# Bias tables built through a DRAM matrix of repeated rows inside the delta rule, and attention run from wide to narrow dilation

## The chip, the cores and the metric

The kernel runs on one core of a Trainium2 chip. The time is device microseconds (us) for one execution. The core has five instruction streams: TensorE (PE, matrix products into PSUM), VectorE (DVE), ScalarE (ACT), GpSimd (POOL) and SyncE (SP). SP and ACT each own a queue on which they issue DMAs; both queues are served by the same 16 DMA engines.

## The reference

One decoder block on 2048 tokens of width 1024, all float32. The change touches two of its parts, which share only their input and are joined by the output projection:

```python
# gated delta rule, 4 heads of 128, a scan over chunks
u = u0_c - w_c @ state;  o = qg_c @ state + aqk_c @ u;  state = gl_c * state + kg_c.T @ u
# attention, 8 heads of 64, three branches (window, dilation) = (128, 1), (512, 4), (2048, 16)
delta = qi + 128 - kj                       # qi < 128, kj < 256
bias = rel_bias[t5_bucket(max(delta, 0) * dil)]
s = q @ k.T * dh ** -0.5 + bias;  s = where(valid, s, -1e30);  o_i, lse_i = softmax parts
ob = sum over branches of softmax(lse) * o_i, then RMSNorm
x = x + gate * (concat([oa, ob]) @ w_out)
```

The bias of a branch depends on `qi - kj` alone: a 128 x 256 table per head whose row is the row above it, shifted by one.

## The kernel before, in words

The program is a row of phases (`PHASES`). Each has its own SBUF tiles and semaphores (`Room`), with a barrier of all engines behind it. The engines follow orders written out by hand and wait on semaphores; there is no scheduler. Four phases matter here.

**The delta rule** (`deltanet`) goes over the 2048 tokens in 16 chunks of 128. SP loads each chunk's operands into two alternating buffers, about one chunk ahead: `nt`, `kg`, `qg`, `aqk`, `vb`, `z` (256 KB each, rows of 2 KB), `kc` (256 KB in rows of 512 B) and eight DMAs of 128-byte rows into the diagonal blocks of `dz` and `dzt` (L941, L942). In chunks 0 to 7 SP also loads 1 MB of the attention's q and k into `big` (L987). For each chunk PE runs eleven groups of 128x128 products (L1023, L1075, L1076), DVE masks and subtracts, ACT copies `u` out of PSUM (L1105) and squares the output, and POOL scales it; SP stores it (L968). The chunks form a chain through `state`.

**The bias tables** (`bias_tables`) come next, as a phase of their own. SP loads the 32x8 bias weights and two constants. One product per branch selects the bucket for each of 384 distances (L1217); DVE adds the mask (L1230), which gives one row of 384 numbers per head and branch, on 8 partitions. The rows go to DRAM in one small DMA (L1207). Three DMAs of 1 MB read them back with the same distance step for each partition, so that the table arrives upside down (L1211); PE turns it over by a product with a flipped identity (L1222), and DVE copies it out of PSUM (L1233).

**Attention** (`attention`) has 48 units of 128 queries, 16 for each branch. `RUNS` sets the order: dilation 1, then 4, then 16. A unit with `False` has 128 keys, one with `True` has 256. POOL gathers strided q and k, SP loads v (L1310, L1313) and stores the unit's output to `o_d` (L1320), and ACT issues the 4 MB load of `w_out` at the start (L1420).

**The output projection** (`mix_out`) reads for each tile of 128 tokens the delta rule's output (`mo_y`) and the three branches' outputs (`mo_o`, 792 KB), weights and normalises them, and multiplies by `w_out`. SP loads tiles 0 and 1 at its start, behind two constants.

Of the kernel before, what the change touches and what calls it, by code (L numbers as in the profile page):

```python
# [880 lines left out]
def deltanet(nc, m, a):  # L881
# [5 lines left out]
    with Room(nc, "gd") as R:  # L887
# [20 lines left out]
        nrm = R.sb("nrm", [P, NT, 2 * GH])  # L908
        pool_self, dve_self = R.plain("pool_self"), R.plain("dve_self")
# [16 lines left out]
        with R.block() as block:  # L926
# [93 lines left out]
            def _(pe):  # L1020
# [57 lines left out]

                fifth_y(0)
# [15 lines left out]
            def _(act):  # L1095
                act.wait_ge(*eps_set.n(1))
                nc.scalar.activation(nrm[:, :, :], m.ssq[:, :, :], ACT.Sqrt, bias=eps[:, :]).then_inc(*nstd_ready.inc)
                act.wait_ge(*nrm_ready.n(2))
                for c in range(NT):
                    b = c % 2  # L1100
                    act.wait_ge(*u_done.n(c + 1))
# [13 lines left out]
                    nc.scalar.activation(st[:, b, :], st[:, b, :], ACT.Sqrt, bias=eps[:, :], scale=1.0 / P).then_inc(*std_ready.inc)  # L1115

            @block.vector
            def _(dve):
# [52 lines left out]

                masked(0, 0, L5)
# [14 lines left out]
def bias_tables(nc, m, a):  # L1187

    with Room(nc, "bt") as R:
        rel = R.sb("rel", [NE, AH])
        hot = R.sb("hot", [NE, NB * BIAS_W])
        off = R.sb("off", [AH, NB * BIAS_W])
        rows = R.sb("rows", [AH, NB * BIAS_W])
        flip = R.sb("flip", [P, NB, AH, 2 * P])
        small_in, rows_out, flip_in = R.sig("small_in", 16), R.sig("rows_out", 16), R.sig("flip_in", 16)
        rows_done, rows_ready, done, read = R.sig("rows_done"), R.sig("rows_ready"), R.sig("done"), R.sig("read")
        ps = m.ps
        with R.block() as block:  # L1200
            @block.sync
            def _(sp):
                sp.dma_start(rel[:, :], a["rel_bias"]).then_inc(*small_in.inc)
                sp.dma_start(hot[:, :], a["bucket_one"]).then_inc(*small_in.inc)
                sp.dma_start(off[:, :], a["bucket_off"]).then_inc(*small_in.inc)
                sp.wait_ge(*rows_ready.n(NB))
                sp.dma_start(m.bias_d, rows[:, :]).then_inc(*rows_out.inc)  # L1207
                sp.wait_ge(*rows_out.n(1))
                for n in range(NB):
                    src = bass.AP(m.bias_d.tensor, n * BIAS_W, [[1, P], [NB * BIAS_W, AH], [1, 2 * P]])  # L1210
                    sp.dma_start(flip[:, n, :, :], src).then_inc(*flip_in.inc)  # L1211

            @block.tensor
            def _(pe):
                pe.wait_ge(*small_in.n(3))
                for n in range(NB):
                    nc.tensor.matmul(ps[0:AH, n, 0:BIAS_W], rel[:, :], hot[:, n * BIAS_W:(n + 1) * BIAS_W], start=True, stop=True).then_inc(*rows_done.inc)  # L1217
                pe.wait_ge(*flip_in.n(NB))
                for n in range(NB):
                    pe.wait_ge(*read.n(n))  # L1220
                    for h in range(0, AH, 2):
                        last = nc.tensor.matmul(ps[:, 4 + h // 2, :], m.cst[:, C_FLIP:C_FLIP + P], flip[:, n, h:h + 2, :].rearrange("p h k -> p (h k)"), start=True, stop=True)  # L1222
                    last.then_inc(*done.inc)

            @block.vector
            def _(dve):
                for n in range(NB):
                    dve.wait_ge(*rows_done.n(n + 1))
                    s = slice(n * BIAS_W, (n + 1) * BIAS_W)
                    nc.vector.tensor_tensor(rows[:, s], ps[0:AH, n, 0:BIAS_W], off[:, s], ALU.add).then_inc(*rows_ready.inc)  # L1230
                for n in range(NB):
                    dve.wait_ge(*done.n(n + 1))
                    nc.vector.tensor_copy(m.bias[:, n, :, :].rearrange("p h k -> p (h k)"), ps[:, 4:8, :].rearrange("p b n -> p (b n)")).then_inc(*read.inc)  # L1233


def attention(nc, m, a):
# [6 lines left out]
        (0, 0, 1, (False,), lambda i, j: 0),  # L1243
        (1, 0, NT // 2 - 1, (True, True), lambda i, j: i * (2 * P) + (1 + j) * P),
        (NT - 1, 0, 1, (True,), lambda i, j: (NT - 1) * P),
        (NT, 1, BR[1][0], (False, True, True, True), lambda i, j: i + j * BR[1][0] * P),
        (2 * NT, 2, BR[2][0] // 2, (False, False), lambda i, j: i * 2 + j),
# [36 lines left out]
    with Room(nc, "at") as R:  # L1284
        qk = m.qk
        qb = R.sb("qb", [P, 2, STEPS, P])
# [7 lines left out]
        later_in = R.sig("later_in", 16)  # L1294
# [5 lines left out]
        with R.block() as block:  # L1300
            @block.sync
            def _(sp):
                for unit, prev in units(sp):
                    if unit:
# [6 lines left out]
                        else:  # L1311
                            src = bass.AP(m.v_d.tensor, first * AW, [[dil * AW, P], [1, AW]])
                            sp.dma_start(v[:, b, 1, :], src).then_inc(*v_in[b].inc)  # L1313
                    if prev:
# [6 lines left out]
                for b in range(2):  # L1321
                    sp.wait_ge(*out[b].n(UNITS // 2))
# [830 lines left out]
class Shared:  # L2153
    pass


def attention_part(nc, m, a):

    with nc.sbuf_tensor("bias", [P, NB, AH, 2 * P], F32) as m.bias:
        bias_tables(nc, m, a)  # L2160
# [99 lines left out]
```

## Time and profile before

| | |
|---|---|
| median of 3 runs | 2684.2 us (2676.27 to 2690.61) |
| profiled execution | 2681.78 us, of it span 2679.9 us |
| PE busy | 2272.5 us (85%) |
| DVE / ACT / POOL busy | 1104.7 / 805.8 / 329.6 us |
| DMA | 426.63 MB, mean 159 GB/s |
| delta rule | from 968 to 1154 us |
| bias tables | from 1155.55 us to 1198.59 us |
| attention | from 1199.3 to 1557 us |
| output projection, first SP issue | 1560.68 us |

The profile gives the time each engine is busy, who released it from a wait, and for the DMAs the number of packets, their bytes, and the share of 16 engines' time that the packets took. In these traces a packet is one contiguous row of a transfer; a DMA adds one small packet per DMA engine used. `issue` as a releaser means that the profile shows nothing that the engine waited for. Times in a timeline are counted from the start of the span.

### The profile page before, as it was taken

How to read it: one execution, taken by the hardware profiler on the slowest of the kernel's cores; microseconds unless marked ns; L12 is line 12 of the kernel's file. 1: busy time of each engine (PE TensorE's matmuls, PEld its weight loads, DVE VectorE, ACT ScalarE, POOL GpSimd, SP SyncE). 2: the span in 40 equal slices, each digit the busy share in tenths (PEclk: the TensorE clock that was granted, in tenths of full speed). 3: DMA queues.
4: the chain of work that ended last, by engine and by line, in shares of the span. 5: the costliest groups of instructions: out<-in, count | busy, mean ns of one | idle time of the engine just before them, and what ended most of it. 6: DMA issues, size and time to landing. Idle time of an engine off the chain costs nothing. (4 is left out here: it accounts for less than half of the span.)

```text
span 2679.9 us, 31777 instructions
## 1 busy us (share of the span) xinstructions
PE 2272.5 (85%) x9218; PEld 1329.4 (50%) x9219; DVE 1104.7 (41%) x2029; ACT 805.8 (30%) x2123; POOL 329.6 (12%) x314
## 2 busy tenths in 40 slices
PE   3999899999888978949999959999169999999940
PEld 2666444444444458926777735555024444444410
DVE  5444132322346525526788845654501111111127
ACT  1433111111333112216777834442011111111125
POOL 0000000000111014411133400000310000000022
PEclk9999999999999989969999979999579999999975
DMA  8443011112456549723233333331058766579767
GB/s 337 146 135 135 33 55 63 55 63 87 137 176 194 176 130 296 237 97 115 95 88 95 104 110 127 127 127 44 5 186 308 242 229 218 202 265 328 270 249 283
DMA packets 178532, 426.63 MB, mean 159 GB/s; under 512 B 41824, under 2 KB 77920, under 8 KB 162960
## 3 DMA queue, kind: packets, MB, share of 16 engines
q1 hardware_dynamic: 153664, 335.37, 36.9%
q0 software_dynamic: 12832, 43.02, 4.7%
q10 hardware_dynamic: 11952, 47.19, 4.3%
q8 instruction: 45, 0.74, 0.1%
q14 instruction: 39, 0.32, 0.0%
HBM read 304.44 MB, written 121.07 MB: 159 GB/s over the span
## 5 line engine op out<-in xcount | busy, mean ns | idle before, releaser
L627 PE MATMUL ps<-big,pc_w 128*128 128x512 f32 x1280 | 556.8, 596 | 10.1 <-DMA pc_w<-in_w_chan 10.1
L627 PEld LDWEIGHTS ps<-big,pc_w 128*128 128x128 f32 x1280 | 243.3, 191 | 310.5 <-issue 299.5
L1976 PE MATMUL ps<-ex_wgu,ex_xt 128*128 x800 | 359.1, 602 | 24.2 <-DMA ex_wgu<-in_w_gate_up 23.5
L1976 PEld LDWEIGHTS ps<-ex_wgu,ex_xt 128*128 128x128 f32 x800 | 150.3, 193 | 198.9 <-issue 198.9
L310 PE MATMUL ps<-cp_wt,big 128*128 128x344 f32 x768 | 225.5, 454 | 0.0
L1562 PE MATMUL ps<-w_out,mo_yt 128*128 128x512 f32 x512 | 225.0, 598 | 0.0
L1372 PE MATMUL ps<-at_v,at_pt 128*128 128x128 f32 (+1 forms) x1200 | 183.1, 290 | 6.2 <-DMA at_v<-v_d 6.2
L1986 PE MATMUL ps<-ex_wd,ex_hidt 128*128 x400 | 181.8, 598 | 4.3 <-issue 2.9
L310 PEld LDWEIGHTS ps<-cp_wt,big 128*128 128x128 f32 x768 | 145.9, 191 | 76.9 <-issue 4.1
L1434 ACT ACTIVATE at_p<-at_p,at_low 128x256 f32<-128x256 f32 (+1 forms) x384 | 174.0, 456 | 20.1 <-DVE at_low L1401 19.7
L1372 PEld LDWEIGHTS ps<-at_v,at_pt 128*128 128x128 f32 x1200 | 149.1, 191 | 52.8 <-issue 35.7
L2058 DVE TENSOR_TENSOR ex_hid<-ex_sg,ps 128x256 f32<-128x256 f32 x50 | 21.1, 421 | 362.1 <-ACT ex_sg L2026 340.1
L1562 PEld LDWEIGHTS ps<-w_out,mo_yt 128*128 128x128 f32 x512 | 97.2, 192 | 116.5 <-issue 116.5
L1399 DVE SCALAR_TENSOR_TENSOR at_p<-ps,bias 128x512 f32<-128x512 f32 (+1 forms) x192 | 109.3, 569 | 69.9 <-PE ps L1347 69.4
L2047 DVE TENSOR_TENSOR ex_y<-ps,mod 128x1024 f32<-128x1024 f32 x50 | 61.2, 1225 | 174.6 <-PE ps L1986 174.6
L2026 ACT ACTIVATE ex_sg<-ps 128x256 f32<-128x256 f32 x50 | 19.3, 386 | 356.7 <-PE ps L1976 356.7
L1347 PE MATMUL ps<-at_kb,at_qb 64*128 64x256 f32 (+1 forms) x768 | 119.5, 389 | 6.1 <-POOL at_kb L1333 5.1
L1949 POOL DMA_INDIRECT ex_xg<-h_d,ex_idx x50 | 47.3, 945 | 545.9 <-DVE ex_idx L2050 499.2
L1417 ACT COPY at_pt<-ps 128x512 f32<-128x512 f32 (+1 forms) x192 | 93.8, 488 | 66.5 <-PE ps L1357 61.1
L782 DVE TENSOR_SCALAR pc_cv<-pc_pre,pc_wc 128x2048 f32<-128x2048 f32 x12 | 15.4, 1287 | 234.5 <-ACT pc_pre L707 234.5
L1401 DVE TENSOR_REDUCE at_low<-at_p 128x2 f32<-128x512 f32 (+1 forms) x192 | 109.4, 570 | 6.6
L1986 PEld LDWEIGHTS ps<-ex_wd,ex_hidt 128*128 128x128 f32 x400 | 72.7, 192 | 78.2 <-issue 78.2
(289 smaller groups left out, 2866.5 us busy)
## 6 DMA issues: line engine op xcount, KB each, us to landing
ex_wgu<-in_w_gate_up SPq DMA_DIRECT2D x32, 2048.0 KB, 11.1
ex_wd<-in_w_down SPq DMA_DIRECT2D x32, 1024.0 KB, 7.8
ys_d<-ex_y ACTq DMA_DIRECT2D x50, 512.0 KB, 8.0
cp_w<-in_w_ada SPq DMA_DIRECT2D x24, 1024.0 KB, 5.4
ch_d<-pc_cv SPq DMA_DIRECT2D x20, 1024.0 KB, 3.9
at_v<-v_d SPq DMA_DIRECT2D x27, 512.0 KB, 3.9
o_d<-at_o SPq DMA_DIRECT2D x48, 264.0 KB, 2.1
mo_o<-o_d SPq DMA_DIRECT2D x16, 792.0 KB, 6.6
```

What stands on the lines that cost most here:

```text
L310: last = nc.tensor.matmul(ps[:, ROW_A + g, 0:THIRD], m.ht[:, k, t * P:(t + 1) * P], wt[:, k, g * THIRD:(g + 1) * THIRD], start=(k == 0), s ...
L627: last = nc.tensor.matmul(ps[:, n % 2, :], w[:, ch % 2, k, :], m.ht[:, k, g * BANK:(g + 1) * BANK], start=(k == 0), stop=(k == KD - 1))
L1347: last = nc.tensor.matmul(ps[:, 2 * (s % 2) + h, lo:2 * P], qb[r, b, s, :], kb[r, b, s, lo:], start=True, stop=True)
L1372: last = nc.tensor.matmul(ps[:, 6 + b, w], pt[:, e, h, k, :], v[:, b, k, w], start=(k == k0), stop=(k == 1))
L1399: nc.vector.scalar_tensor_tensor(p[:, s, :, lo:], ps[:, 2 * e:2 * e + 2, lo:2 * P], DH ** -0.5, m.bias[:, unit[0][1], 2 * s:2 * s + 2, lo: ...
L1401: nc.vector.tensor_reduce(low[:, b, 2 * s:2 * s + 2], p[:, s, :, lo:], AX.X, ALU.max, negate=True).then_inc(*max_ready[e].inc)
L1417: nc.scalar.copy(pt[:, e, :, k:, :], ps[:, 4 + e, :].rearrange("p (h k n) -> p h k n", h=2, k=2)[:, :, k:, :]).then_inc(*pt_ready[e].inc)
L1434: ins = nc.scalar.activation(p[:, s, h, lo:], p[:, s, h, lo:], ACT.Exp, bias=low[:, b, at:at + 1], accum_out=low[:, b, at + AH:at + AH + 1])
L1562: last = nc.tensor.matmul(ps[:, 2 + 2 * b + n, :], yt[:, b, k, :], w[:, k, n * BANK:(n + 1) * BANK], start=(k == 0), stop=(k == KD - 1))
L1976: last = nc.tensor.matmul(ps[:, 2 + b, :], xt[:, b, k, :], wgu[:, bass.ds(half * WGU + k * 2 * DE, 2 * DE)], start=(k == 0), stop=(k == KD ...
L1986: last = nc.tensor.matmul(ps[:, 6 + n, :], hidt[:, b, k, :], wd[:, bass.ds(half * WD + (k * D + n * BANK), BANK)], start=(k == 0), stop=(k ...
L2047: nc.vector.tensor_tensor(y[:, b, :], ps[:, 6:8, :].rearrange("p n w -> p (n w)"), gate, ALU.mult).then_inc(*y_ready[b].inc)
```

## The change

The bias phase goes. Its work moves into the delta rule, and the turning over by PE and DVE is replaced by DRAM traffic: `bias_d` grows from one row per head and branch to 128 copies of it (3 x 8 x 128 x 384 floats, 4.72 MB), written by ACT from 8 partitions. A read whose step from partition to partition is one less than the row length then takes from each copy a window that starts one element earlier, and gives the table the right way up; ACT issues these three reads (1 MB each) ahead of chunks 5, 6 and 7. The tables lie in an SBUF tile that lives from the delta rule to the output projection; it holds the constants and rows first.

```diff
 deltanet, PE, in read_state and ahead of fifth_y(0):
+                    if c == 0:
+                        pe.wait_ge(*rows_ready.n(NB))
+                def bias_rows():
+                    pe.wait_ge(*table_in.n(3))
+                    for n in range(NB):
+                        last = nc.tensor.matmul(ps[0:AH, KS + n, 0:BIAS_W], rel[:, :], hot[...], start=True, stop=True)
+                    last.then_inc(*rows_done.inc)
+                bias_rows()
                 fifth_y(0)
 deltanet, ACT:
+                act.dma_start(rel[:, :], a["rel_bias"]).then_inc(*table_in.inc)
+                act.dma_start(hot, a["bucket_one"]).then_inc(*table_in.inc)
+                act.dma_start(off, a["bucket_off"]).then_inc(*table_in.inc)
                 nc.scalar.activation(nrm[:, :, :], m.ssq[:, :, :], ACT.Sqrt, bias=eps[:, :])
+                act.wait_ge(*rows_ready.n(NB))
+                for n in range(NB):
+                    act.dma_start(m.bias_d[n], rows[:, n * BIAS_W:(n + 1) * BIAS_W].unsqueeze(1).to_broadcast([AH, P, BIAS_W])).then_inc(*rows_out.inc)
                 for c in range(NT):
+                    if 5 <= c < 5 + NB:
+                        act.wait_ge(*rows_out.n(NB))
+                        src = bass.AP(m.bias_d.tensor, (c - 5) * AH * P * BIAS_W + P - 1, [[BIAS_W - 1, P], [P * BIAS_W, AH], [1, 2 * P]])
+                        act.dma_start(bias[:, c - 5, :, :], src).then_inc(*bias_in.inc)
                     act.wait_ge(*u_done.n(c + 1))
 deltanet, DVE, ahead of masked(0, 0, L5):
+                dve.wait_ge(*rows_done.n(1))
+                for n in range(NB):
+                    nc.vector.tensor_tensor(rows[:, s], ps[0:AH, KS + n, 0:BIAS_W], off[:, s], ALU.add).then_inc(*rows_ready.inc)
-def bias_tables(nc, m, a): ...
 attention:
-        (0, 0, 1, (False,), ...), (1, 0, NT // 2 - 1, (True, True), ...), (NT - 1, 0, 1, (True,), ...),
+        (0, 2, BR[2][0] // 2, (False, False), ...),
         (NT, 1, BR[1][0], (False, True, True, True), ...),
-        (2 * NT, 2, BR[2][0] // 2, (False, False), ...),
+        (2 * NT, 0, 1, (False,), ...), (2 * NT + 1, 0, NT // 2 - 1, (True, True), ...), (3 * NT - 1, 0, 1, (True,), ...),
 attention, SP, ahead of the last unit's store:
+                    if not unit:
+                        for b in range(2):
+                            sp.wait_ge(*out[b].n(UNITS // 2 - 1))
+                            sp.dma_start(m.my[:, b, 0:GW], m.y_d[b]).then_inc(*tile_in.inc)
+                            sp.dma_start(m.mo[:, b, :, :], ...).then_inc(*tile_in.inc)
 ...
+                sp.wait_ge(*tile_in.n(4))
 mix_out:
-                load_y(0, 0, 0)
-                load_y(1, 1, 0)
 block_kernel:
-        m.bias_d = dram("bias_d", [AH, NB * BIAS_W])
+        m.bias_d = dram("bias_d", [NB, AH, P, BIAS_W])
```

On ACT, at the start of the delta rule, the program had before:

```order
L1097 ACT_TABLE_LOAD
L1097 ACTIVATE gd_nrm<-ssq,gd_eps 128x128
L1105 COPY gd_u<-ps 128x512
L1111 ACTIVATE gd_o,gd_st<-ps,gd_nrm 128x128 x4
L1113 COPY gd_o<-ps 128x512
```

and has now (`bias` is the shared tile; `gd_u` is the first chunk's `u`):

```order
L1111 DMA gd_rel<-in_rel_bias 32x8
L1112 DMA bias<-in_bucket_one 32x1152
L1113 DMA bias<-in_bucket_off 8x1152
L1115 ACT_TABLE_LOAD
L1115 ACTIVATE gd_nrm<-ssq,gd_eps 128x128
L1119 DMA bias_d<-bias 1024x1x384 x3
L1131 COPY gd_u<-ps 128x512
```

Six DMAs moved ahead of the first `u` copy, three of them with 1024 rows of 384 floats each. Before chunk 5 (and likewise 6 and 7) ACT now has one more DMA, behind a wait for the three writes:

```order
L1139 COPY gd_o<-ps 128x512
L1141 ACTIVATE gd_st<-gd_st,gd_eps 128x4
L1126 DMA bias<-bias_d 128x8x256
L1131 COPY gd_u<-ps 128x512
L1137 ACTIVATE gd_o,gd_st<-ps,gd_nrm 128x128 x4
```

The read stands ahead of the `u` copy, on which the rest of the chunk depends. On SP, from the last units of attention to the output projection, the program had before:

```order
L1320 DMA o_d<-at_o 128x528
L1300 UNCONDITIONAL_BRANCH
L1502 UNCONDITIONAL_BRANCH
L1504 DMA mo_gain<-in_attn_norm 128x512
L1505 DMA mo_wr<-in_w_router 128x288
L1509 DMA mo_y<-y_d 128x512
L1511 DMA mo_o<-o_d 128x3x528
```

and has now (`mod` and `mo` hold tiles 0 and 1):

```order
L1301 DMA mod<-y_d 128x512
L1302 DMA mo<-o_d 128x3x528
L1301 DMA mod<-y_d 128x512
L1302 DMA mo<-o_d 128x3x528
L1309 DMA o_d<-at_o 128x528
L1283 UNCONDITIONAL_BRANCH
L1490 UNCONDITIONAL_BRANCH
L1492 DMA mo_gain<-in_attn_norm 128x512
L1493 DMA mo_wr<-in_w_router 128x288
```

The four tile loads moved from behind the barrier to ahead of the last unit's store.

## Rows read from the trace of the kernel before

**Rows 1.** Stretches: length, busy time per engine, granted clock, DMA share, GB/s.

```profile
core 0: us, PE busy (x) PEld busy (x) DVE busy (x) ACT busy (x) POOL busy (x), PEclk, DMA share, GB/s
987.00:1079.00 92.00, 84.75 (x702) 82.72 (x701) 50.25 (x128) 24.04 (x97) 36.15 (x32) 0.96 0.90 289
1079.00:1152.00 73.00, 62.39 (x516) 60.03 (x515) 39.23 (x100) 20.22 (x81) 35.11 (x31) 0.96 0.64 196
1155.00:1199.00 44.00, 18.28 (x30) 6.21 (x30) 8.51 (x6) 0.00 (x0) 0.00 (x0) 0.67 0.25 77
1199.00:1218.00 19.00, 10.40 (x44) 6.55 (x44) 5.85 (x12) 7.25 (x27) 4.30 (x6) 0.55 0.66 263
```

**Rows 2.** Timeline, ACT in the delta rule: start, duration, instruction, [idle before <-releaser].

```profile
987.92 0.59 ACT L1105 COPY gd_u<-ps 128x512 f32<-128x512 f32 x1 [18.36 <-PE ps L1023]
...
1035.43 0.33 ACT L1115 ACTIVATE gd_st<-gd_st,gd_eps 128x4 f32<-128x4 f32 x1
1040.53 0.59 ACT L1105 COPY gd_u<-ps 128x512 f32<-128x512 f32 x1 [4.77 <-PE ps L1023]
...
1132.61 0.59 ACT L1105 COPY gd_u<-ps 128x512 f32<-128x512 f32 x1 [2.69 <-PE ps L1023]
1141.94 0.59 ACT L1105 COPY gd_u<-ps 128x512 f32<-128x512 f32 x1 [2.68 <-PE ps L1023]
```

**Rows 3.** Timeline, PE in the delta rule, products that read `dz`.

```profile
976.80 2.05 PE L1023 MATMUL ps<-gd_dz,gd_nt 128*128 128x128 f32 x8 [15.42 <-DMA gd_dzt<-xtb_d]
...
1016.09 1.52 PE L1023 MATMUL ps<-gd_dz,gd_nt 128*128 128x128 f32 x8 [2.39 <-issue]
1038.47 1.13 PE L1023 MATMUL ps<-gd_dz,gd_nt 128*128 128x128 f32 x8 [2.10 <-issue]
```

**Rows 4.** Timeline, the bias phase and the start of attention.

```profile
1155.55 0.35 SPq L1203 DMA_DIRECT2D bt_rel<-in_rel_bias  x1
1156.41 0.60 SPq L1205 DMA_DIRECT2D bt_off<-in_bucket_off  x1
1159.03 4.00 PE L1217 MATMUL ps<-bt_hot,bt_rel 32*8 32x384 f32 x6 [12.98 <-DMA bt_off<-in_bucket_off]
1160.51 0.55 DVE L1230 TENSOR_TENSOR bt_rows<-ps,bt_off 8x384 f32<-8x384 f32 x1 [11.09 <-PE ps L1217]
...
1199.30 0.40 ACTq L1420 DMA_DIRECT2D w_out<-in_w_out  x1
1201.13 0.35 SPq L1313 DMA_DIRECT2D at_v<-v_d  x1
1212.82 1.22 PE L1372 MATMUL ps<-at_v,at_pt 128*128 128x128 f32 x4 [6.19 <-DMA at_v<-v_d]
```

**Rows 5.** DMA queue 1, 1164.3:1164.7 (`bias_d<-bt_rows`): packets, MB, share of 16 engines.

```profile
q1 hardware_dynamic: 7, 0.03, 62.2%
```

**Rows 6.** The same, 1152.8:1152.9 (`y_d<-gd_o`, from 128 partitions).

```profile
q1 hardware_dynamic: 20, 0.04, 106.0%
```

**Rows 7.** Packets by size, 1163:1165.4 (`bias_d<-bt_rows` alone).

```profile
DMA packets 16, 0.04 MB, mean 15 GB/s; under 512 B 8, under 2 KB 8, under 8 KB 16
```

**Rows 8.** The queues, 1204:1210: q10 carries `w_out`, q1 the first `at_v`.

```profile
q10 hardware_dynamic: 66, 2.16, 83.7%
q1 hardware_dynamic: 60, 0.12, 5.3%
```

**Rows 9.** Queue 1 in 968:1152, in 979:1000, in 979:1002, and in 1163:1180.

```profile
q1 hardware_dynamic: 44160, 43.86, 76.1%
q1 hardware_dynamic: 5599, 5.61, 86.5%
q1 hardware_dynamic: 6827, 6.00, 85.8%
q1 hardware_dynamic: 3136, 3.18, 60.1%
```

**Rows 10.** Timeline, the end of attention and the start of the output projection.

```profile
1552.31 3.02 SPq L1320 DMA_DIRECT2D o_d<-at_o  x2
1560.68 0.35 SPq L1504 DMA_DIRECT2D mo_gain<-in_attn_norm  x1
1568.24 0.17 DVE L1580 TENSOR_TENSOR mo_lo<-mo_o 128x8 f32<-128x8 f32 x1 [10.02 <-DMA mo_o<-o_d]
```

**Rows 11.** Queue 1 in 1557.5:1572, the first loads of the output projection.

```profile
q1 hardware_dynamic: 1520, 3.08, 63.0%
```

More of the change, by code:

```diff
@@ L908, in deltanet @@
         nrm = R.sb("nrm", [P, NT, 2 * GH])
+        rel = R.sb("rel", [NE, AH])
+        wide = NB * BIAS_W
+        hot, off, rows = m.bias[0:NE, 0:wide], m.bias[0:AH, wide:2 * wide], m.bias[0:AH, 2 * wide:3 * wide]
+        bias = m.bias[:, :].rearrange("p (n h k) -> p n h k", n=NB, h=AH)
+        table_in, rows_out, bias_in = R.sig("table_in", 16), R.sig("rows_out", 16), R.sig("bias_in", 16)
+        rows_done, rows_ready = R.sig("rows_done"), R.sig("rows_ready")
         pool_self, dve_self = R.plain("pool_self"), R.plain("dve_self")
@@ L1077, in outputs @@
                     last.then_inc(*o_done.inc)
+                def bias_rows():
+                    pe.wait_ge(*table_in.n(3))
+                    for n in range(NB):
+                        last = nc.tensor.matmul(ps[0:AH, KS + n, 0:BIAS_W], rel[:, :], hot[:, n * BIAS_W:(n + 1) * BIAS_W], start=True, stop=True)
+                    last.then_inc(*rows_done.inc)
+                bias_rows()
                 fifth_y(0)
@@ L1186, in _ @@
                 reciprocals(NT - 1)
[L1187 to L1233, printed above, removed]
@@ L1285, in attention @@
         qk = m.qk
+        bias = m.bias[:, :].rearrange("p (n h k) -> p n h k", n=NB, h=AH)
         qb = R.sb("qb", [P, 2, STEPS, P])
@@ L1473, in mix_out @@
         eps = R.sb("eps", [P, 1])
-        y = R.sb("y", [P, 2, 2 * GW])
-        o = R.sb("o", [P, 2, NB, OW])
-        x = R.sb("x", [P, 2, D])
+        y, o = m.my, m.mo
+        x, h, ht = (m.bias[:, n * 2 * D:(n + 1) * 2 * D].rearrange("p (b n) -> p b n", b=2) for n in range(3))
+        ht = ht.rearrange("p b (k n) -> p b k n", k=KD)
         wt = R.sb("wt", [P, 2, NB, AH])
@@ L1578, in put_together @@
                     low = o[:, b, :, AW:AW + AH]
-                    dve.wait_ge(*tile_in[b].n(2 * q + 2))
+                    if not is_tile(q, 0):
+                        dve.wait_ge(*tile_in[b].n(2 * q))
                     link(nc.vector.tensor_tensor(lo[:, b, :], low[:, 0, :], low[:, 1, :], ALU.min))
@@ L2154 @@
     pass
-def attention_part(nc, m, a):
-    with nc.sbuf_tensor("bias", [P, NB, AH, 2 * P], F32) as m.bias:
-        bias_tables(nc, m, a)
-        attention(nc, m, a)
-PHASES = (condition_and_project, project_channels, deltanet, attention_part, mix_out, route, experts, finish)
+PHASES = (condition_and_project, project_channels, deltanet, attention, mix_out, route, experts, finish)
 def block_kernel(nc, a, out):
@@ L2210, in block_kernel @@
         m.x2 = big[:, :].rearrange("p (t n) -> p t n", n=D)
-        for phase in PHASES[:3]:
+        for phase in PHASES[:2]:
             phase(nc, m, a)
-        with nc.sbuf_tensor("w_out", [P, KD, D], F32) as m.w_out:
-            for phase in PHASES[3:5]:
-                phase(nc, m, a)
+        with nc.sbuf_tensor("bias", [P, NB * AH * 2 * P], F32) as m.bias:
+            deltanet(nc, m, a)
+            with ExitStack() as held:
+                m.w_out = held.enter_context(nc.sbuf_tensor("w_out", [P, KD, D], F32))
+                m.my = m.mod[:, 0:2 * D].rearrange("p (b n) -> p b n", b=2)
+                m.mo = held.enter_context(nc.sbuf_tensor("mo", [P, 2, NB, AW + 2 * AH], F32))
+                for phase in PHASES[3:5]:
+                    phase(nc, m, a)
         for phase in PHASES[5:]:
```

17 lines of the change are left out of this document (9 added, 8 removed).

## The prediction

> **What bounds the kernel now.** I read the page's slices first (PE is busy nearly everywhere; a short dip stands between the delta rule and attention), then the busy time by stretch, then the timeline of the dip, and last the DMA queues, because the change moves traffic onto them. In the bias phase PE is busy 18 of 44 us, DVE 8.5, ACT and POOL not at all, and the DMA share is 0.25 [rows 1]: nothing in it is a bound, it is latency after latency. The delta rule is the opposite. Chunks 0 to 8 have PE busy 85 of 92 us and the DMA engines 0.90 of the time; the last chunks have the DMA at 0.64 [rows 1]. The copies of `u` show the pace: 9.33 us a chunk where nothing is late (the last two), 154.0 us for the 15 steps from first to last [rows 2], so 154.0 - 15 x 9.33 = 14 us are already lost, and the two places where PE idles over 2 us ahead of a product that reads `dz` [rows 3] say to what: blocks of `dz` and `dzt` that land late, behind the other loads of a full queue. So the change takes serial latency away and puts traffic into the one stretch whose DMA is nearly full.
>
> **What it removes.** SP's first issue of the bias phase is at 1155.55, that of attention at 1201.13 [rows 4]. Both stand behind the same barrier, so the phase is worth 45.6 us. I take 45. Attention still begins with the wait for its first v, which lands behind the 4 MB of `w_out` (PE idle until 1212.82, granted clock 0.55 until 1218, between the levels of 1.2 and 2.4 GHz) [rows 1, 4]; nothing of that goes.
>
> **What it adds on the engines: nothing.** The constants are issued by ACT right at the start of the delta rule, at about 968. In the bias phase 2.0 us passed from the last of these issues to the first product, the products took 4.0 us and each of three adds 0.55 [rows 4]. So the rows are ready near 968 + 1.2 + 2.0 + 4.0 + 1.7 = 977, and PE, which waits for `dzt` until 976.80 [rows 3], has finished by then. DVE's first real operand comes behind that product. ACT's first copy of `u` is at 987.92, after 18 us of idling [rows 2], and covers the three writes' issue. If this cover were gone it would cost 2 us.
>
> **The writes.** Three DMAs of 1024 rows of 384 floats leave from 8 partitions. The nearest row is the small store of the same rows: 16 packets, 8 of them small, so 8 DMA engines with one data packet each [rows 7]. Seven of its packets of 4608 B took 0.622 x 0.4 x 16 / 7 = 0.57 us each [rows 5]. Packets of 2048 B from 128 partitions took 1.06 x 0.1 x 16 / 20 = 0.085 us [rows 6]. Per byte that is 0.123 against 0.041 ns: reading from 8 partitions with 8 engines runs at a third of the speed. A row of 1536 B then takes 0.19 us (0.064 at full speed). Each of the 8 engines gets 3 x 129 = 387 packets: 73.5 us of its time at the slow rate, 24.8 at the fast one. I take the slow one; it is the only row with this shape. The Trainium skill, in "SBUF — State Buffer", section "Door 1: The DMA port swizzle", lists partitions 0 to 3 on one DMA port and 4 to 7 on another, at about 27 GB/s each; by that the 4.72 MB would take an estimated 87 us, and the store's packets fit it (4608 B at a quarter of 27 GB/s is 0.68 us, 0.57 measured).
>
> **What the writes do to SP's loads.** They go through the same engines. How two queues share one is seen where `w_out` and the first v run together: 66 packets of the one, 60 of the other in 6 us, though the one kind is 32 KB and the other 2 KB [rows 8]. An engine takes a packet from each in turn, so a queue of small packets waits out the other's slow ones. In the delta rule SP's mean packet takes 0.761 x 184 x 16 / 44160 = 0.051 us [rows 9]. From about 979 on, the 8 engines alternate: 387 x (0.19 + 0.051) = 93 us, until 1072, for 387 of SP's packets each, 6192 over 16 engines. Before, SP had that many through between 1000 and 1002 [rows 9], by 1001. The lag is 71 us. If the slow rate comes from all eight reading at once, a packet gets up to a fifth shorter while others are in SP's packets: 387 x (0.152 + 0.051) - 22 = 57. I take 64. The stretch is bound by DMA, PE's own 9.33 us per chunk [rows 2] cannot win it back, and each load is needed by the chunk after next at the latest. The Trainium skill says the same of the turns in "DMA: Bandwidth & Descriptors", section "Queues, rings and completion order" (each DMA engine goes round its queues a packet at a time); it does not say whether a read that waits holds up the other queue, and that is what decides.
>
> **The reads.** The three reads have the shape of the flipped ones, whose 3136 packets took 0.601 x 17 = 10.2 us of all engines [rows 9]. The three chunks they fall in leave about a tenth of 30 us free [rows 1]: 7 us, with 0 (they fall into time lost anyway) and 10 as bounds. Attention first needs a table after chunk 15.
>
> **The edges of attention.** Units of dilation 16 come first: all units are the same as before, only their order changes, so I charge the strided first gather with 1 us. At the end the last unit now has 256 keys, and its products drain some 1.6 us later. The four tile loads (2.1 MB; before, 3.08 MB of such loads took 0.63 x 14.5 = 9.1 us [rows 11], so 6.3 us) start about 4 us ahead of the last store, which lands behind them, some 2.3 us late. In return the output projection no longer waits for its tile: before, DVE starts 7.6 us after SP's first issue there [rows 10]; now it waits only for the two constants, about 3 us (two issues, and the 2.0 us to land of rows 4). Gain 4.5, loss 3.9, and the gather's 1: with rounding I take +1, between -4 and +4.
>
> Sum: -45 + 64 + 7 + 1 = +27 on the profiled execution's 2681.8 us: 2709 us. That execution lies 2.4 us under the median of the three runs, which is less than they scatter. Between the bounds of this case (57 and 71 for the lag, 0 and 10, -4 and +4): 2690 to 2723; with the estimated 87 us in place of 73.5 it would be some 14 us more.
>
> **Rival A, faster: the slow reads do not hold up the other queue,** or packets of 1536 B are not slow in a stream. Then the writes cost the engines only their bytes, 24.8 us on eight of them, of which the free tenth of 70 us covers 7: 18 us. They end by 979 + 73.5 = 1052 even at the slow rate, about when ACT reaches the wait ahead of chunk 5 (1035.43 before [rows 2], plus the 18). Sum -45 + 18 + 7 + 1 = -19: 2663 us, 2655 with the chunk time regained, 2675 if the wait decides with the 87 us. For it: data from one slow source need not block an engine. Against it: the shares of rows 5 to 8 are those of packets that follow each other, never side by side.
>
> **Rival B, no change: the ACT queue does not take 387 packets per engine at once.** The 192 of the flipped reads were taken. The rest, 195 x 0.24 = 47 us, would hold ACT until 1026 where the first `u` is due at 987.92: 38 us. If the loads are otherwise unhindered, -45 + 38 + 7 + 1 = +1: 2683 us. Under the forecast's mechanism it hides behind the lag.
>
> **Rival C: the gain of the removed phase is not there,** since attention's start merely inherits the stall. Nothing speaks for it: both engines' first issues stand behind the barrier [rows 4]. It would give 2709 + 45 = 2754.
>
> **Chances.** Forecast 0.49, A 0.40, B 0.08, C and the rest 0.03. The measurement of this kernel tells about 0.5% (13.4 us) from no change. A lies below that nearly whole, the forecast above it nearly whole: faster 0.40, same 0.10, slower 0.50. Since both signs hold much, the range reaches from 2656 to 2728, and the forecast's own is 2690 to 2728.
>
> **What would show it.** Right: in the delta rule the copies of `u` of chunks 1 to 3 lie 20 to 45 us apart with PE waiting ahead of the products that read `dz`, queue 10 has some 3100 packets of about 0.19 us there, and from chunk 5 on the pace is 9.3 to 13 us; the delta rule takes 240 to 265 us instead of 186. Wrong: chunks 1 to 4 at 10 to 13 us; then either ACT idles ahead of chunk 5's copy on the writes (A at the slow rate) or does not (A at the fast one). A first `u` copy later than 1000 with ACT's issues ahead of it would be B. For the edges: the first DVE instruction of the output projection some 7 us behind the end of attention, not 11.

## The result and the profile after

| | before | changed |
|---|---|---|
| median | 2683.78 us (2676.27 to 2690.61, 5 runs) | 2727.63 us (2726.67 to 2766.22, 5 runs) |
| profiled execution, span | 2679.9 us | 2764.4 us |
| ratio of the times | | 1.020, 95% interval 1.013 to 1.027 |

By the medians the changed kernel is slower by 44 us; the forecast was slower by 27. The ratio counts all five executions and gives 53 us; whether the loss is above 2% stays open within its interval. The profiled execution happens to be the longest of the five, 2766.22 us; the other four lie between 2726.67 and 2732.24, and without it the means differ by 46 us. So what is particular to it has to be kept apart from what the change does (last part of this section). In the experiments the ratio, unlike the medians and ranges, leaves out executions far above the others of the same version.

The stretches of the delta rule, columns as in [rows 1]:

```profile
976.00:1070.00 94.00, 20.61 (x128) 19.80 (x128) 10.09 (x22) 2.76 (x11) 4.56 (x4) 0.61 0.55 91
1070.00:1152.00 82.00, 67.60 (x525) 66.01 (x526) 37.43 (x94) 17.15 (x67) 27.43 (x24) 0.89 0.94 304
1152.00:1230.00 78.00, 73.15 (x622) 70.61 (x620) 45.55 (x119) 22.72 (x92) 37.67 (x33) 1.00 0.75 230
```

While nearly all of the writes run (976 to 1070), PE is busy 21 of 94 us and the DMA engines move 91 GB/s, where before they moved 289 [rows 1]. A DMA share of 0.55 with so few bytes says that packets take long, not that there is little to move.

The timeline of ACT, which answers to [rows 2]:

```profile
976.09 42.52 ACTq L1119 DMA_DIRECT2D bias_d<-bias  x3
1029.61 0.58 ACT L1131 COPY gd_u<-ps 128x512 f32<-128x512 f32 x1 [59.34 <-PE ps L1029]
1077.34 0.59 ACT L1131 COPY gd_u<-ps 128x512 f32<-128x512 f32 x1 [41.09 <-PE ps L1029]
1086.88 0.58 ACT L1131 COPY gd_u<-ps 128x512 f32<-128x512 f32 x1 [2.91 <-PE ps L1029]
...
1226.63 0.58 ACT L1131 COPY gd_u<-ps 128x512 f32<-128x512 f32 x1 [2.69 <-PE ps L1029]
...
1238.43 0.36 ACTq L1410 DMA_DIRECT2D w_out<-in_w_out  x1
```

The copies of `u` of chunks 0 to 2 come at 1029.61, 1077.34 and 1086.88. The third copy of before, two steps of 9.2 and 9.3 us behind its first at 987.92 [rows 2], was at 1006.44: 80.4 us are lost by then. The last copy is at 1226.63 against 1141.94 [rows 2], 84.7 us later. `w_out` is issued at 1238.43 against 1199.30 [rows 4], 39.1 us later: the 84.7 less 45.6 of the removed phase. That is nearly the whole result.

PE on the products that read `dz`, which answers to [rows 3], with the product of the bias rows ahead of them:

```profile
970.48 4.00 PE L1090 MATMUL ps<-bias,gd_rel 32*8 32x384 f32 x6 [9.94 <-SPq L160]
976.37 0.55 PE L1029 MATMUL ps<-gd_dz,gd_nt 128*128 128x128 f32 x1 [1.88 <-issue]
...
1025.90 2.05 PE L1029 MATMUL ps<-gd_dz,gd_nt 128*128 128x128 f32 x8 [39.22 <-issue]
...
1073.57 2.05 PE L1029 MATMUL ps<-gd_dz,gd_nt 128*128 128x128 f32 x8 [35.60 <-issue]
```

The constants and the small product cost nothing: the first `dz` product stands at 976.37 (before 976.80). The loss lies ahead of the two later ones. The profile puts `issue` there and names no releaser; what is late in that time is to be seen in SP's own timeline, which issues the loads of `dz`:

```profile
977.41 0.43 SPq L939 DMA_DIRECT2D gd_nt<-nt_d  x1
977.88 3.96 SPq L947 DMA_DIRECT2D gd_dz<-xb_d  x1
981.88 3.83 SPq L948 DMA_DIRECT2D gd_dzt<-xtb_d  x1
...
1066.14 3.64 SPq L947 DMA_DIRECT2D gd_dz<-xb_d  x1
1069.82 1.81 SPq L948 DMA_DIRECT2D gd_dzt<-xtb_d  x1
1071.74 0.38 SPq L955 DMA_DIRECT2D gd_kc<-ch_d  x1
```

Until the writes begin an issue takes 0.43 us; from 977.88 to 1070 nearly every one takes about 4 us; from 1071.74 on 0.4 again. The issues stand back to back, so SP waits for nothing else in the program there. The queues in 976 to 1070:

```profile
q10 hardware_dynamic: 3058, 4.67, 41.4%
q1 hardware_dynamic: 4692, 3.89, 13.9%
```

and queue 1 in the same stretch of the kernel before:

```profile
q1 hardware_dynamic: 24768, 26.37, 88.9%
```

Queue 10's packets took 0.414 x 94 x 16 / 3058 = 0.204 us each. In 94 us queue 1 passed 4692 packets, a fifth of before: SP's own queue hardly moves, and that its issues are long for this reason is read from the two standing together.

**The output projection,** which answers to [rows 10]:

```profile
1637.94 0.43 SPq L1301 DMA_DIRECT2D mod<-y_d  x1
...
1642.14 0.35 SPq L1309 DMA_DIRECT2D o_d<-at_o  x1
1650.51 0.33 SPq L1492 DMA_DIRECT2D mo_gain<-in_attn_norm  x1
1650.89 0.42 SPq L1493 DMA_DIRECT2D mo_wr<-in_w_router  x1
1655.05 0.17 DVE L1567 TENSOR_TENSOR mo_lo<-mo 128x8 f32<-128x8 f32 x1 [6.63 <-DMA mo_wr<-in_w_router]
```

DVE starts 4.5 us behind SP's first issue (7.6 before), and what it waits for are now the constants.

**What only this execution shows.** From `w_out` to DVE's first instruction of the output projection it took 416.6 us, against 368.9 before. The rows by stretch say why:

```profile
1238.00:1258.00 20.00, 11.32 (x52) 8.14 (x54) 5.64 (x14) 7.65 (x30) 6.02 (x6) 0.50 0.59 237
1258.00:1378.00 120.00, 120.00 (x566) 90.91 (x565) 64.98 (x141) 64.50 (x282) 29.02 (x29) 0.54 0.19 62
1378.00:1642.00 264.00, 260.86 (x1954) 200.24 (x1953) 209.94 (x326) 194.64 (x651) 69.30 (x62) 1.00 0.31 96
```

For 120 us PE was busy without a gap and the granted clock was 0.54 in the mean, that is nearly all of it at 1.2 GHz instead of 2.4. The experiments come back to this.

### The profile page after: what moved, and what is told of

Read it like the earlier page. It is cut to its first block and busy times, and to the rows that moved or that the text cites. A ratio compares the mean times of both kernels' runs of the same rounds, so it can differ in the third digit from the quotient of the medians.

```text
span 2764.4 us, 31703 instructions
## 1 busy us (share of the span) xinstructions
PE 2311.6 (84%) x9194; PEld 1366.2 (49%) x9195; DVE 1101.3 (40%) x2026; ACT 804.9 (29%) x2123; POOL 328.9 (12%) x314
## 5 line engine op out<-in xcount | busy, mean ns | idle before, releaser
L1362 PE MATMUL ps<-at_v,at_pt 128*128 128x128 f32 (+1 forms) x1200 | 207.1, 316 | 5.2 <-DMA at_v<-v_d 5.2
L1362 PEld LDWEIGHTS ps<-at_v,at_pt 128*128 128x128 f32 x1200 | 168.9, 213 | 56.1 <-issue 47.0
L1337 PE MATMUL ps<-at_kb,at_qb 64*128 64x256 f32 (+1 forms) x768 | 133.8, 432 | 13.1 <-POOL at_kb L1323 12.0
L1347 PE MATMUL ps<-cst,at_p 128*128 128x128 f32 x600 | 110.7, 300 | 1.5 <-ACT at_p L1424 1.5
L1946 PE MATMUL ps<-cst,ex_xg 128*128 128x128 f32 x400 | 54.0, 280 | 68.4 <-DMA ex_xg<-h_d,ex_idx 66.0
```

Source lines behind the costliest of these rows:

```text
L1337: last = nc.tensor.matmul(ps[:, 2 * (s % 2) + h, lo:2 * P], qb[r, b, s, :], kb[r, b, s, lo:], start=True, stop=True)
L1347: last = nc.tensor.transpose(ps[:, 4 + e, (h * 2 + k) * P:(h * 2 + k + 1) * P], p[:, s, h, k * P:(k + 1) * P], m.ident)
L1362: last = nc.tensor.matmul(ps[:, 6 + b, w], pt[:, e, h, k, :], v[:, b, k, w], start=(k == k0), stop=(k == 1))
```

## The experiments

The ratio is always to the kernel before, timed beside it. Where a text on record speaks of the narrow dilation coming first, it means the changed kernel's order, and the word is wrong: that order begins with dilation 16, the widest.

### The changed kernel once more

No edit.

> The changed kernel once more, unaltered, with a profile of its own. In its first profiled execution (2766 us) TensorE ran at the lower clock (granted 0.50) through the first 130 us of attention; the other four executions took 2727 to 2732 us. If that clock was a matter of that one execution, this profile shows attention at 1.00 from about 15 us after its start, a time near 2727, and the copies of u in the delta rule at the same offsets as before (the last one about 259 us after the start of the delta rule). If the long idling in the delta rule brings the low clock with it, attention is slow again and the profile is near 2766.

Measured: 2722.95 us (2718.08 to 2732.99, 4 runs) against 2681.28; ratio 1.017 (1.014 to 1.020). The writes' issue took 43.17 us, the last copy of `u` came at 1225.04, and from `w_out` (1236.83) to the output projection (1608.66) it took 371.8 us. The clock came back early:

```profile
1257.00:1307.00 50.00, 49.89 (x366) 38.51 (x366) 37.88 (x92) 41.58 (x182) 19.29 (x19) 0.92 0.30 97
1307.00:1597.00 290.00, 285.72 (x2149) 219.49 (x2148) 230.23 (x375) 217.04 (x748) 79.48 (x72) 1.00 0.32 98
```

So the lag in the delta rule is there again (the third copy of `u` came at 1086.49, 80 us late), and the 120 us at the low clock are not a trait of every execution.

### The same packets from spread partitions

```diff
-  hot, off, rows = m.bias[0:NE, 0:wide], m.bias[0:AH, wide:2 * wide], m.bias[0:AH, 2 * wide:3 * wide]
+  hot, off, rows = m.bias[0:NE, 0:wide], m.bias[0:4 * AH, wide:2 * wide], m.bias[0:4 * AH, 2 * wide:3 * wide]
...
-  act.dma_start(m.bias_d[n], rows[:, ...].unsqueeze(1).to_broadcast([AH, P, BIAS_W]))
+  act.dma_start(m.bias_d[n], rows[0:4 * AH:4, ...].unsqueeze(1).to_broadcast([AH, P, BIAS_W]))
```

The eight rows stand on partitions 0, 4, ..., 28 instead of 0 to 7. Packets, bytes, order and the eight engines stay. (`rel_bias` is spread with a DVE copy, so that the product puts them there; with this copy and two memsets the writes begin 3 us later.)

> The eight rows lie on partitions 0, 4, 8, ..., 28 in place of 0 to 7; the three writes still have 3072 packets of 1536 B and still run on 8 DMA engines. Theory one (eight engines read neighbouring partitions through too few ways out of SBUF): a packet takes 0.065 us in place of 0.20, the writes end within 45 us of their issue, the delta rule gets 55 to 65 us shorter, the time is 2660 to 2675 us. Theory two (a DMA on 8 engines is slow whatever its partitions are): packets stay at 0.20 us and the time at 2727. Theory three (the cost is that 387 packets per engine are queued at once, at whatever rate): ACT's issue stays blocked for tens of us and the time stays above 2700.

Measured: 2689.56 us (2655.17 to 2722.42, 6 runs); three at 2655 to 2670, three at 2710 to 2722; ratio 0.993 (0.989 to 0.997). The queues in 979 to 1020, where the writes now fall, and ACT's timeline:

```profile
q1 hardware_dynamic: 7507, 6.82, 52.1%
q10 hardware_dynamic: 3096, 4.72, 30.5%
```

```profile
979.09 18.37 ACTq L1122 DMA_DIRECT2D bias_d<-bias  x3
997.50 0.59 ACT L1134 COPY gd_u<-ps 128x512 f32<-128x512 f32 x1 [24.08 <-issue]
...
1161.17 0.59 ACT L1134 COPY gd_u<-ps 128x512 f32<-128x512 f32 x1 [2.69 <-PE ps L1030]
```

A packet takes 0.305 x 41 x 16 / 3096 = 0.065 us, a third of 0.204, and queue 1 passes 7507 packets in 41 us instead of 4692 in 94. The last copy of `u` is 19 us later than before instead of 85. Of the writes themselves nothing but the place of the source differs, so the place is the cause (theory one). Theory two is out by the packets, theory three by the time: ACT is still held for 18.37 us with 387 packets an engine, and the last copy of `u` comes 65 us sooner than in the changed kernel all the same. The Trainium skill agrees ("SBUF — State Buffer", section "Door 1: The DMA port swizzle"): by its table partitions 0 to 7 lie on two ports and 0, 4, ..., 28 on eight. In the changed kernel the writes passed 4.7 MB from 976 to 1072, 49 GB/s or 25 on each of the two ports; the Trainium skill has about 27 for one port in the same section.

### Rows on all 128 partitions

```diff
-  act.dma_start(m.bias_d[n], rows[:, ...].unsqueeze(1).to_broadcast([AH, P, BIAS_W]))
+  act.dma_start(m.bias_d[n].rearrange("h (c j) k -> (h c) j k", j=AH),
+                rows[:, ...].unsqueeze(1).to_broadcast([P, 8, BIAS_W]))
```

The product gives each head's row on 16 partitions; all 16 DMA engines take part.

> The rows are computed on all 128 partitions (16 copies of each head's row), so the writes have the same 3072 packets of 1536 B but come from 128 partitions on 16 DMA engines. Theory one: packets of 0.065 us, 192 per engine, 12.5 us of DMA time; the delta rule costs 20 us over before (12.5 for the writes and 10 for the reads, less the free tenth), the time is 2655 to 2670 us, a few us under the one with 8 spread partitions. Theory two gives the same here, so this run shows what full spreading is worth, and the two together tell partitions from engines. Theory three: 192 per engine still block the queues in part, above 2690.

Measured: 2655.31 us (2647.04 to 2695.20, 4 runs), ratio 0.989 (0.986 to 0.992): 26 us under before. The issue takes 4.25 us instead of 42.52, the last copy of `u` is at 1158.89, 17 us later than before. A packet takes 0.069 us (3120 packets, 61.0% of 22 us). What is left goes with ordinary traffic in a full stretch: the DMA share from 1020 to 1090 is 0.99.

### One write at a time

```diff
-  for n in range(NB):
-      act.dma_start(m.bias_d[n], rows[:, n * BIAS_W:(n + 1) * BIAS_W]...)
   for c in range(NT):
+      if c in (0, 4, 8):
+          act.dma_start(m.bias_d[c // 4], rows[:, c // 4 * BIAS_W:(c // 4 + 1) * BIAS_W]...)
-      if 5 <= c < 5 + NB:
+      if 12 <= c < 12 + NB:
```

> The three writes from partitions 0 to 7 are issued one at a time, ahead of chunks 0, 4 and 8, and the reads ahead of chunks 12, 13 and 14. If slow packets hold up SP's loads packet by packet, each write costs its own share of the lag wherever it stands: 80 / 3 = 27 us each for the first two, less for the third (the DMA is 0.64 busy there), 65 to 80 us in all, and the time is 2710 to 2727. If the cost is in the number queued at once (129 per engine are taken without blocking), the lag falls under 30 us and the time is 2670 to 2685.

Measured: 2722.56 us (2718.38 to 2749.51, 5 runs), ratio 1.015 (1.013 to 1.017). Now ACT is held by none of its issues:

```profile
975.59 0.82 ACTq L1121 DMA_DIRECT2D bias_d<-bias  x1
1013.80 0.59 ACT L1131 COPY gd_u<-ps 128x512 f32<-128x512 f32 x1 [43.97 <-PE ps L1029]
...
1050.69 0.70 ACTq L1121 DMA_DIRECT2D bias_d<-bias  x1
1054.96 0.59 ACT L1131 COPY gd_u<-ps 128x512 f32<-128x512 f32 x1 [3.64 <-PE ps L1029]
1091.23 0.59 ACT L1131 COPY gd_u<-ps 128x512 f32<-128x512 f32 x1 [29.46 <-PE ps L1029]
...
1118.38 0.67 ACTq L1121 DMA_DIRECT2D bias_d<-bias  x1
1122.18 0.59 ACT L1131 COPY gd_u<-ps 128x512 f32<-128x512 f32 x1 [3.16 <-PE ps L1029]
1158.49 0.59 ACT L1131 COPY gd_u<-ps 128x512 f32<-128x512 f32 x1 [29.50 <-PE ps L1029]
```

The same steps of the kernel before, from the fifth copy to the sixth and from the ninth to the tenth, were these:

```profile
1029.11 0.59 ACT L1105 COPY gd_u<-ps 128x512 f32<-128x512 f32 x1 [2.69 <-PE ps L1023]
1040.53 0.59 ACT L1105 COPY gd_u<-ps 128x512 f32<-128x512 f32 x1 [4.77 <-PE ps L1023]
...
1073.21 0.59 ACT L1105 COPY gd_u<-ps 128x512 f32<-128x512 f32 x1 [2.69 <-PE ps L1023]
1085.32 0.59 ACT L1105 COPY gd_u<-ps 128x512 f32<-128x512 f32 x1 [5.45 <-PE ps L1023]
```

Each write delays the chunk behind it: the first `u` by 25.9 us, and the two long steps are 36.3 us where they were 11.4 and 12.1, 24.9 and 24.2 more. Together 75 us. The last copy, with the reads in it, is 77.7 us later than before, against 84.7 with three writes at once. SP's issues take 3.1 to 4.5 us while a write runs here too. So neither the depth of ACT's queue nor the time that ACT is held decides, but the slow packets by themselves: a write has 129 per engine, and its packets took 0.200, 0.184 and 0.186 us (1032 packets with 32.2%, 29.7% and 30.0% of the 40 us from 975, 1050 and 1118), which makes 25.8, 23.8 and 24.0 us.

This version's profiled execution is also its longest, 2749.51 us: in attention the granted clock is 0.50 from 1253 to 1313 with PE busy all the time.

### Repeating from DRAM, early

```diff
-  for n in range(NB):
-      act.dma_start(m.bias_d[n], rows[...].unsqueeze(1).to_broadcast([AH, P, BIAS_W]))
+  act.dma_start(m.rows_d, rows)
   for c in range(NT):
+      if c == 1:
+          act.wait_ge(*rows_out.n(1))
+          for n in range(NB):
+              src = bass.AP(m.rows_d.tensor, n * BIAS_W, [[0, P], [NB * BIAS_W, AH], [1, BIAS_W]])
+              act.dma_start(m.bias_d[n].rearrange("h p k -> p h k"), src)
```

> The two bias rows of four heads are written once to a small DRAM tensor (4 partitions, 3 KB each), and three copies from DRAM to DRAM, issued by ACT ahead of chunk 1 of the delta rule, repeat them into bias_d; the reads stand ahead of chunks 5, 6 and 7 as in the changed kernel. Same bytes into bias_d, but no packet read out of few neighbouring partitions save the first 12 KB. Theory one (the source in a few neighbouring partitions makes packets slow, and SP's packets on the same 8 engines wait for them): q10's share in 968:1160 is near the 13% of the version with 128 partitions, the last gd_u copy ends near 1159 and the time is 2650 to 2665. Theory two (writing bias_d in 1.5 KB packets is slow whatever the source): q10's share stays near 26%, the last gd_u copy comes near 1220 and the time is 2710 to 2730.

(The rows stand on eight partitions, one for each head, with 4.6 KB each; the text on record says four heads and 3 KB by mistake.)

Measured: 2664.01 us (2660.51 to 2718.46, 4 runs) against 2679.22, ratio 0.993 (0.990 to 0.996). Queue 10 has 13.1% of 968 to 1160, and the last copy of `u` is at 1161.56, 20 us later than before. Theory one again: same bytes, same packets into `bias_d`, no slow source, and three quarters of the lag gone.

### Repeating from DRAM, late

```diff
-      if c == 1:
+      if c == 9:
...
-      if 5 <= c < 5 + NB:
+      if 12 <= c < 12 + NB:
```

> As the previous one, with the copies ahead of chunk 9 and the reads ahead of chunks 12, 13 and 14, where the kernel before keeps the DMA engines 64% busy instead of some 90%. If what is left of the cost (17 us at the last gd_u copy with 128 partitions) is DMA time that the copies take from loads on which the delta rule waits, it goes here: last gd_u copy at 1142 to 1150 and the time 2640 to 2655. If it is a delay of loads behind the copies, whenever they come, the last gd_u copy is again near 1159 and the time near 2655.

Measured: 2667.75 us over 10 runs, six from 2644.70 to 2677.00, four from 2695.03 to 2723.02; ratio of the six 0.991 (0.988 to 0.994). The last copy of `u` is at 1153.20: 6 to 8 us better than the early ones and 3 us short of what I expected. The slack of the late chunks takes up a part of the traffic, not all: around the copies two steps are 15 and 16 us.

### The order of attention alone

```diff
   # delta rule and bias phase as before the change; from the change only:
-  (0, 0, 1, (False,), lambda i, j: 0),
-  (1, 0, NT // 2 - 1, (True, True), lambda i, j: i * (2 * P) + (1 + j) * P),
-  (NT - 1, 0, 1, (True,), lambda i, j: (NT - 1) * P),
+  (0, 2, BR[2][0] // 2, (False, False), lambda i, j: i * 2 + j),
...
+  sp.dma_start(m.my[:, b, 0:GW], m.y_d[b]).then_inc(*tile_in.inc)
+  sp.dma_start(m.mo[:, b, :, :], m.o_d[:, b, :, :].rearrange("n p w -> p n w")).then_inc(*tile_in.inc)
```

> The delta rule and the bias phase of the kernel before, and only the attention of the changed one: narrow dilation first, output tiles loaded in it, the other mix_out. My forecast of the edges alone is +1 us (bounds -4 to +4): 2680 to 2690. Rival: the new order lengthens the attention itself, by its loads or by a granted clock that stays at 0.50 longer after the pause of PE: then the time is 2690 to 2710 and the attention, from the issue of w_out to the last issue of o_d, is longer than the 355.7 us of before.

Measured: 11 runs, seven from 2674.80 to 2690.07 and four from 2731.92 to 2745.83; ratio of the seven 1.001 (0.999 to 1.003). Both expectations hold, each for a part of the executions. The profile is of one of the four:

```profile
1217.00:1337.00 120.00, 120.00 (x534) 90.84 (x534) 63.26 (x133) 60.84 (x266) 27.57 (x27) 0.51 0.18 58
1337.00:1600.00 263.00, 260.55 (x1949) 199.08 (x1948) 211.77 (x330) 195.88 (x660) 70.61 (x64) 1.00 0.30 94
```

It is the picture of the changed kernel's profiled execution: 120 us of unbroken work at 1.2 GHz, in a kernel whose delta rule is untouched. The edit also brings the four tile loads and the buffers they go to; the loads are issued at the end of attention, long behind the stretch at the low clock.

### The old order with the changed delta rule

The reverse: the changed kernel with the five entries of the order, the tile loads and waits of before (the diff above backwards).

> The changed kernel's delta rule, with its writes and reads of bias tables, and the attention of the kernel before (its order and loads). If the edges are worth nothing this takes as long as the changed kernel, 2715 to 2730, the last gd_u copy at 1225 and the attention 356 us. If the order of attention costs something by itself, or brings executions in which the granted clock stays at 0.50, this is 5 to 30 us below the changed kernel.

Measured: 2719.02 us (2714.63 to 2723.79, 4 runs), ratio 1.013 (1.011 to 1.015). The last copy of `u` is at 1227.98. Where no execution is at the low clock, the edges are worth nothing that these runs can tell.

### The late copies with the old order

Both edits together: the late copies from DRAM to DRAM, and attention as before.

> The delta rule of the version with late copies from DRAM to DRAM (ahead of chunk 9, reads ahead of 12, 13 and 14) and the attention of the kernel before. That version had its last gd_u copy at 1153 (before 1142) and executions of 2645 to 2659 us, but also four of ten at 2695 to 2723 us. If the low granted clock in attention goes with the narrow dilation coming first, every execution here lies at 2640 to 2662 with the median near 2650, 30 us under before. If it has another cause (the shorter pause of PE ahead of attention), some executions are again 40 us or more above the rest.

Measured: 2653.28 us (2644.48 to 2658.51, 5 runs) against 2685.41; ratio 0.988 (0.985 to 0.990). Its rows in the timeline and the stretches:

```profile
1151.22 0.58 ACT L1136 COPY gd_u<-ps 128x512 f32<-128x512 f32 x1 [2.86 <-PE ps L1030]
1164.35 0.35 ACTq L1408 DMA_DIRECT2D w_out<-in_w_out  x1
```

```profile
1164.00:1184.00 20.00, 11.57 (x52) 7.44 (x52) 6.59 (x14) 7.85 (x29) 4.30 (x6) 0.52 0.62 250
1184.00:1304.00 120.00, 120.00 (x897) 91.87 (x896) 90.07 (x141) 88.25 (x281) 22.95 (x28) 1.00 0.29 93
```

`w_out` is issued 34.95 us earlier than before [rows 4]: 45.6 of the removed phase less 9.3 of lag, and 1.4 where the delta rule ends and attention starts. The first 120 us behind the pause have 897 products here, 566 and 534 in the pictures at the low clock above. This is the version to keep: faster than both kernels, with all its runs within 14 us.

### 128 partitions with the old order

> The version with the rows on 128 partitions, written from all of them ahead of chunk 0, with the attention of the kernel before. Its last gd_u copy came at 1159, 6 us behind that of the late copies, so by the delta rule it should take about 2655 us, 6 us more than the kernel it is compared with here. With the old order of attention no execution is expected 40 us above the rest; if some are, the order of attention is not what brings the low clock.

The rows on 128 partitions, and attention as before.

Measured: 2656.32 us (2652.51 to 2660.97, 5 runs), ratio 0.989 (0.987 to 0.991). The last copy of `u` is at 1155.67. This version and the late copies are not told apart by their intervals; no execution is at the low clock.

**All executions by the order of attention.** With dilation 16 first, 49 executions of seven kernels: 16 lie 30 us or more above the fastest of their kernel (31 to 78 us; among them the 2677.00 of the late copies), each with a mean granted clock below that of its fellows. Three of the 16 have a profile, and all three show the low clock at the start of attention. With the order of before, 42 executions of the kernel before and 14 of three others: none is more than 23 us above its fastest. That attention in its new form brings these executions is shown, by the order alone in one direction and by its removal in the other. What in it does so is not. (The last two versions were timed on another chip than those with the new order; the 33 executions of the kernel before that were timed beside the new order have none.) In both orders PE waits for its first v and is at 0.50 to 0.57 of the clock in the first 20 us; what differs is the work that follows, units of dilation 16 with 128 keys each. The first 120 us behind the pause, in an undisturbed execution (the late copies with the new order), against the row of 1184 to 1304 above:

```profile
1185.00:1305.00 120.00, 118.56 (x911) 90.37 (x910) 99.67 (x205) 100.80 (x411) 50.26 (x42) 1.00 0.31 98
```

DVE and ACT are busy 100 and 101 us instead of 90 and 88, and PE has 1.4 us of gaps where the old order has none. Whether that matters is open; nothing inside the order was tried.

## Why the prediction came out as it did

Direction, place and cause were right: slower, in the delta rule, from slow packets of queue 10 that hold up the loads of queue 1. The size was short by 17 us by the medians (27 against 44), and by the ratio of all executions the loss, 53 us, is twice the forecast. Term by term:

| term | forecast | measured |
|---|---|---|
| phase removed | -45 | -45.6 |
| constants, product, adds | 0 | 0 (976.37 against 976.80) |
| lag from the writes | +64 | +80.4 |
| reads | +7 | +4.3 |
| edges of attention | +1 | 0 to +3, in a third of the executions with the new order 31 to 78 more |
| sum | +27 | +39 at `w_out`, 39 to 42 with the edges, +44 in the medians |

**The step that failed is the lag of the writes,** the term of +64, which measured +80.4. Three things in it were off, all to the low side.

- I had 71 us and took 64, because a slow packet might get shorter while other engines are in packets of SP. It did not: 0.204 us in a stream of 3058. 7 us.
- The price of a packet was 0.19 us, from seven packets in 0.4 us [rows 5]. Over 387 packets the difference to 0.204 is 5 us of an engine's time.
- I let one SP packet pass for each slow one, 387 on each engine. The trace has 303: queue 1 passed 4855 packets from 976 to 1072. By 1072, when the last writes are through, queue 1 is where it was at 991.5 before, 80.5 us earlier; my count had 1072 against 1001. The two rows:

```profile
q1 hardware_dynamic: 6295, 4.37, 14.7%
```

of the changed kernel in 968 to 1072, and of the kernel before in 968 to 991.5:

```profile
q1 hardware_dynamic: 6291, 4.37, 64.3%
```

Price and count together are the 9.5 us from 71 to 80.5. The end of the writes, 1072, was forecast to the microsecond, but by luck: they began 3 us earlier, their packets were slower, and fewer of SP's passed between them. One row of each queue in turn was my reading of [rows 8], and I took it for what the Trainium skill says of the turns. But the Trainium skill, in "DMA: Bandwidth & Descriptors", section "Queues, rings and completion order", speaks of packets of some 9 to 17 descriptors, and how these fall on the rows that the traces count, no run here shows. The prediction's estimate of 87 us from the Trainium skill (4.72 MB through two ports at about 27 GB/s, "SBUF — State Buffer", section "Door 1: The DMA port swizzle") is to be set against the 96 us that the writes lasted, and not against the engines' own 79.

The sum has a simpler form: in a stretch bound by DMA, the lag is near the slow packets' own time on their engines, 387 x 0.204 = 79 us of the 80.4, as SP's packets have to pass anyway and cancel. The one-by-one run bears it out for each write, 24 to 26 us calculated and lost. With fast packets it is an upper bound: from spread partitions 387 x 0.065 = 25 us, where the third copy of `u` (1024.73 against 1006.44) is 18 us late.

**The second step is the edges.** What the forecast left out altogether is that attention in its new order lets the clock stay low in about a third of the executions, 31 to 78 us each: I priced the first gather and the last unit, and not what comes between them, as all units were the same. One of the five executions behind the table's ratio is of this kind. Why the clock stays low is open.

**The signs.** PE did wait ahead of the products that read `dz`, with 3096 packets of 0.20 us on queue 10. The loss was placed one chunk too late: the first copy of `u` is already 41.7 us late and one step is 47.7 us, where I had the copies of chunks 1 to 3 lie 20 to 45 us apart. The delta rule takes some 271 us (186 and the 84.7), above the 240 to 265 forecast. And the forecast's upper bound, -45 + 71 + 10 + 4, makes 2722, not 2723.

**Rival A** (slow reads don't hold up the other queue) had 0.40 and is refuted: SP's issues at 4 us, and its packets at a fifth of the pace, stand beside 3058 packets of 0.204 us. Its number, though, is nearly that of the versions with a fast source: it forecast 2663 with 25 us for writes and reads, and the versions with 128 partitions and with early copies from DRAM show 17 and 20 us at the last copy of `u`, and 2655 and 2664 us.

**Rival B** was right on its fact and wrong on its worth. ACT was held by its issues for 42.52 us, until 1018.61 (forecast until 1026), so they were not covered by ACT's idling as the prediction had it, and B's sign, a first `u` later than 1000 with ACT's issues ahead of it, was there. But `u` came only at 1029.61, by PE's wait for a product that began at 1025.90, so nothing hung on ACT; and with one write at a time, ACT free, 75 us were lost all the same. The sign did not tell B from the forecast.

**Rival C** is refuted: from the last copy of `u` to `w_out` it took 57.4 us before and 11.8 after, so the whole 45.6 us were gained.

**The reads**: from the third copy of `u` to the last, 139.75 us against 135.50 before, so 4.3. **The ends of attention**: DVE of the output projection waits for the constants, as forecast, and starts 3.0 us earlier behind SP's first issue where 4.5 were forecast. From `w_out` to that instruction it took 368.9 us before and 371.8 in the repeated run of the changed kernel; the order alone gives a ratio of 1.001.

## What to carry to other kernels

A DMA that repeats a few rows costs little more than its bytes only if the source is spread: put the rows on partitions four apart or on all 128, or let DRAM be the source; here all 128 turned +42 us into -26. Look for slow packets of one queue where another queue's *issues* get longer, and price their damage in a stretch bound by DMA as their number per engine times their duration, with no discount. Time a new order of work in ten executions rather than three before trusting a median: an effect that strikes one in three can hide in a small sample.

## What was not expected of the hardware

- The hold-up reaches the issuing engine. SP's issues rose from 0.43 to about 4 us beside packets of 0.204 us, although SP's own packets were small and had other sources. The length is not set by the rows of the DMA being issued: one of 512 rows (`kc`, at 1010.49) took 4.03 us like those of 128.
- More than one slow packet passes for each of SP's. From 990 to 1010 the eight engines with writes passed 679 / 8 = 85 slow ones each, and the 16 engines 659 / 16 = 41 of SP's in the mean, two to one; over the whole of the writes it is 387 to 303. Why is open.

```profile
q10 hardware_dynamic: 679, 1.03, 45.3%
q1 hardware_dynamic: 659, 0.09, 2.7%
```

- The number of engines mattered little beside the number of places in SBUF: eight engines from spread partitions had packets of 0.065 us, sixteen from all 128 partitions 0.069, DRAM to DRAM 0.068 to 0.072.
- With PE busy without a gap for 120 us, the granted clock could stay at 0.50 to 0.54; in the repeated run of the changed kernel it was back within 10 us of the same point of attention (0.50 until 1264, 0.94 from 1264 to 1270). Such executions came with the new order of attention (16 of 49 against 0 of 56), and their cause stays open.
